# Retention layer: turns, scores, moments and gate products set as steps between the weight units, output units in another order

## The reference, cut to what matters

```python
proj = x @ w_in                            # 1024 -> q 1024, k 1024, v 2048, g 2048
q = rotary(q, pos); k = rotary(k, pos) * dk ** -0.5        # 4 heads of 256
out = decayed_scores(q, k) @ v             # 4 heads of 512, causal, decay by distance
mu, var = mean(out), mean(square(out - mu))                # per token and head
normed = (out - mu) * rsqrt(var + eps) * gn_g
y = silu(g) * normed
return y @ w_out                           # 2048 -> 1024
```

## Times and profile before

| what | value |
|---|---|
| three runs | 2921.59 us median (2919.26 to 2927.62) |
| profiled execution | 2919.76 us, span 2917.9 us |
| PE busy | 2676.1 us, 92% |
| DVE busy | 2125.4 us, 73% |
| ACT busy | 1609.9 us, 55% |
| granted TensorE clock, mean | 0.962 of full speed |
| weights and other data moved | 666 MB, 228 GB/s over the span |

### The profile page before, as it was taken

The page is one execution under the profiler, slowest core; times in us unless marked ns, Lnnn a source line. Parts: engine busy times, 40 slices in busy tenths (PEclk is TensorE's granted clock), DMA queues, the critical chain, the costliest instruction groups (busy, mean ns, idle before and its releaser), DMA issues.

```text
span 2917.9 us, 39530 instructions
## 1 busy us (share of the span) xinstructions
PE 2676.1 (92%) x12842; PEld 2166.2 (74%) x12842; DVE 2125.4 (73%) x2500; ACT 1609.9 (55%) x2092; POOL 19.9 (1%) x37
## 2 busy tenths in 40 slices
PE   3989989988989999998999888699999999999997
PEld 2767768876767787766898667588878877888885
DVE  6766567776656755855545865689989989989998
ACT  2554444445444444433344544477767777777775
POOL 0000000000000000000000000000000000000000
PEclk9999999998999999999999879799999999999999
DMA  6655458755544565644555420599989999999995
GB/s 233 223 155 166 157 180 264 248 188 166 176 146 152 188 194 165 212 130 141 168 180 173 147 80 30 201 333 344 355 300 363 332 351 331 352 342 334 364 358 206
DMA packets 357967, 666.04 MB, mean 228 GB/s; under 512 B 23008, under 2 KB 57312, under 8 KB 357200
## 3 DMA queue, kind: packets, MB, share of 16 engines
q1 hardware_dynamic: 354080, 648.51, 66.2%
q0 software_dynamic: 3760, 15.91, 1.7%
HBM read 663.29 MB, written 1.05 MB: 228 GB/s over the span
## 4 chain that ended last, share of the span: by engine, by line
PE 80%; DVE 8%; ACT 5%; issue 3%; DVEq 2%; DMA 1%; ACTq 0%; SPq 0%
PE ps L451 44%; PE ps L457 22%; DVE wlo L1884 2%; PE ps L471 2%; PE ps L562 2%; ACT whi L1320 1%; PE ps L476 1%; DVE mod_sum L1908 1%; PE ps L1223 1%; PE ps L661 1%; DMA raw<-in_w_ada 1%; DMA ada_raw<-in_w_ada 1%; PE ps L773 1%; DVEq L1907 0%; PE ps L631 0%
## 5 line engine op out<-in xcount | busy, mean ns | idle before, releaser
L1884 DVE TENSOR_TENSOR wlo<-raw,whi 128x1024 fp32r<-128x1024 f32 x709 | 863.5, 1224 | 469.7 <-ACT whi L1320 459.6
L1320 ACT ACTIVATE whi<-raw 128x1024 fp32r<-128x1024 f32 x709 | 746.8, 1059 | 737.8 <-PE ps L457 630.7
L451 PE MATMUL ps<-whi,xh 128*128 128x512 f32 (+3 forms) x1248 | 457.8, 377 | 12.8 <-issue 9.0
L451 PE MATMUL ps<-whi,xl 128*128 128x512 f32 (+3 forms) x1248 | 445.3, 367 | 0.0
L451 PE MATMUL ps<-whi,gathered_hi 128*128 128x512 f32 x896 | 361.8, 404 | 3.4 <-DVE att L2158 2.6
L451 PE MATMUL ps<-whi,gathered_lo 128*128 128x512 f32 x896 | 355.1, 396 | 0.0
L457 PE MATMUL ps<-wlo,xh 128*128 128x512 f32 (+3 forms) x1248 | 294.6, 363 | 0.0
L457 PE MATMUL ps<-wlo,gathered_hi 128*128 128x512 f32 x896 | 283.4, 397 | 5.4 <-DVE wlo L1884 5.4
L451 PEld LDWEIGHTS ps<-whi,xh 128*128 128x128 f32 x1248 | 241.3, 193 | 56.0 <-issue 14.4
L451 PEld LDWEIGHTS ps<-whi,xl 128*128 128x128 f32 x1248 | 241.5, 193 | 37.3 <-issue 1.9
L457 PEld LDWEIGHTS ps<-wlo,xh 128*128 128x128 f32 x1248 | 217.0, 192 | 38.5
(11 more groups left out here) (390 smaller groups left out, 3577.4 us busy)
## 6 DMA issues: line engine op xcount, KB each, us to landing
raw<-in_moe_w_in SPq DMA_DIRECT2D x227, 512.0 KB, 5.5
spare<-in_moe_w_in SPq DMA_DIRECT2D x165, 512.0 KB, 5.7
mod_b<-in_moe_w_out SPq DMA_DIRECT2D x165, 512.0 KB, 5.4
raw<-in_w_ff SPq DMA_DIRECT2D x128, 512.0 KB, 4.6
raw<-in_w_in SPq DMA_DIRECT2D x96, 512.0 KB, 4.0
work<-in_moe_w_in SPq DMA_DIRECT2D x56, 512.0 KB, 5.6
work<-in_moe_w_out SPq DMA_DIRECT2D x56, 512.0 KB, 5.3
raw<-in_w_ada SPq DMA_DIRECT2D x48, 512.0 KB, 4.8
```

Source lines behind the costliest of these rows:

```text
L451: e.matmul(ps[0:lhs[2], banks[t], at:at + width], part[:, k0 + j, t * P:t * P + lhs[2]], whi[:, slot, w], start=first and j == 0 and part ...
L1320: e.activation(whi[:, slot, :], src, ACT.Copy).then_inc(split_hi, 1)
L1884: e.tensor_tensor(wlo[:, slot, :], src, whi[:, slot, :].bitcast(F32), ALU.subtract).then_inc(split_lo, 1)
```

## The change

Nothing of the arithmetic is changed. The instructions of stages 2 and 4 get numbers of weight units behind which they run. With `values` the first v unit, `gated` the first gate unit, `projected` the first output unit:

```diff
+                values = c.n.get("unit", 0) + 16
+                gated, projected = values + 16, values + 32
 PE:
+                at(values + 1, source)
+                at(values + 9, source)
+                for i in range(4):
+                    at(values + 1 + i, wide_turn(0, 2 * i))
+                    at(values + 9 + i, wide_turn(D, 2 * i))
+                at(values + 14, scores)
+                at(gated + 13, source, out_turn(0))
+                at(gated + 14, out_turn(4))
+                at(projected + 4, source, out_turn(8))
+                at(projected + 8, source, out_turn(12))
 ACT:
+                for i in range(4):
+                    at(values + 2 + i, wide_copy(qT, 2 * i))
+                    at(values + 10 + i, wide_copy(kT, 2 * i))
+                at(gated + 8, lambda e: root(e, 8))
+                at(gated + 14, turned(0))
+                at(gated + 15, turned(4))
+                at(projected + 5, turned(0))
+                at(projected + 9, turned(4))
 DVE (the copies and the four turned as in ACT):
+                at(values + 15, decayed)
+                at(gated + 9, inverse)
+                at(gated + 10, gate(0))
+                at(gated + 11, gate(1))
+                at(gated + 14, turned(0), gate(2))
+                at(projected + 1, gate(3))
```

What else changes on PE: `clear` ahead of the turns, ahead of the scores and behind the products with v is gone, and so is ACT's `vec` there. The products with v wait for the chunk before the last only, and for the last one ahead of head 3:

```diff
-                clear(e)
-                chunks_read(e)
...
                 source(e)
+                e.wait_ge(evac_act, c.at("chunk", 1))
+                e.wait_ge(evac_dve, c.at("chunk", 1))
                 for h in range(RET_H):
...
+                    if h == RET_H - 1:
+                        chunks_read(e)
                     job(e, tile0)
                     job(e, tile1)
-                clear(e)
                 for _ in range(4):
                     chunk(e, X, NT, D)
```

The output units come column half 1 first, so that the first unit writes banks 4 and 5, and only the second one waits for ACT's reading of the last gate chunk (banks 2 and 3). SP loads in the same order:

```diff
+RET_OUT = [(kg, n) for kg in range(6) for n in (1, 0)]
...
+                turned(e)
+                for i, (kg, n) in enumerate(RET_OUT):
+                    if i == 1:
+                        chunks_read(e)
+                    if i == 8:
+                        turned(e)
+                    unit(e, Y, NT, kg % 4 * UROWS, (2 + 2 * n, 3 + 2 * n), UCOLS, kg == 0, False)
+                turned(e)
```

More of the change, by code:

```diff
@@ L1039, in retention, with at, wide_turn, fill @@
                 X, Y = (xh, xl, P), (yh, yl, P)
+                values = c.n.get("unit", 0) + 16
+                gated, projected = values + 16, values + 32
+                def at(i, *pieces):
+                    c.weave.setdefault(i, []).extend(pieces)
+                def wide_turn(base, b):
+                    def fill(e, bank):
+                        for j in range(2):
+                            for t in range(NT):
+                                tr = e.transpose(ps[:, bank, (j * NT + t) * P:(j * NT + t + 1) * P],
+                                                 proj[:, t, base + (b + j) * P:base + (b + j + 1) * P], ident)
+                        return tr
+                    return lambda e: side_job(e, fill)
+                def scores(e):
+                    clear(e)
+                    for h in range(RET_H):
+                        for b in range(2):
+                            e.matmul(ps[:, 4 + h // 2, (h % 2) * S:(h % 2 + 1) * S], kT[:, 2 * h + b, 0:P],
+                                     qT[:, 2 * h + b, :], start=b == 0, stop=b == 1)
+                    for h in range(RET_H):
+                        for b in range(2):
+                            mm = e.matmul(ps[:, 7, h * P:(h + 1) * P], kT[:, 2 * h + b, P:S],
+                                          qT[:, 2 * h + b, P:S], start=b == 0, stop=b == 1)
+                    mm.then_inc(score_ready, 1)
+                    c.add("job_d")
+                def out_turn(first):
+                    return lambda e: side_turn(e, lambda t, b: ret_O[:, t, (first + b) * P:(first + b + 1) * P], 4)
+                at(values + 1, source)
[8 more added lines that the diff above has]
+                at(projected + 8, source, out_turn(12))
                 first_chunk(e, lambda t, b: x[:, t, b * P:(b + 1) * P], X)
@@ L1682, in retention, with at, wide_copy, turned @@
             def retention(e):
+                values = c.n.get("unit", 0) + 16
+                gated, projected = values + 16, values + 32
+                def at(i, *pieces):
+                    c.weave.setdefault(i, []).extend(pieces)
+                def wide_copy(dst, b):
+                    return lambda e: jobs(e, [plain(dst[:, b:b + 2, :], lambda bank: ps[:, bank, :].rearrange("p (h s) -> p h s", h=2))])
+                def turned(first):
+                    return lambda e: turn(e, yh[:, first:first + 4, :], 4)
+                for i in range(4):
[6 more added lines that the diff above has]
+                at(projected + 9, turned(4))
                 for side in range(4):
@@ L1696, in retention @@
                     chunk(e, D, read)
[L1697 to L1701, removed]
+                pass_units(e, len(RET_OUT))
                 layer_norm_roots(e, 4)
@@ L2538, in view, with at, wide_copy, turned @@
+                gated, projected = values + 16, values + 32
+                def at(i, *pieces):
+                    c.weave.setdefault(i, []).extend(pieces)
                 def view(t, h):
                     return ret_O[:, t, h * 512:(h + 1) * 512]
+                def wide_copy(dst, b):
+                    return lambda e: jobs(e, [plain(dst[:, b:b + 2, :], lambda bank: ps[:, bank, :].rearrange("p (h s) -> p h s", h=2))])
+                def turned(first):
+                    return lambda e: turn(e, yh[:, first:first + 4, :], yl[:, first:first + 4, :], 4)
@@ L2564, in retention, with inverse @@
[L2564 to L2567, removed]
+                        if i == NT * RET_H - 1:
+                            e.tensor_scalar(st[:, 0:8], st[:, 64:80].rearrange("p (i k) -> p i k", k=2)[:, :, 1], LN_EPS, None, ALU.add)
+                            to_act(e)
+                    return piece
+                def inverse(e):
+                    from_act(e)
+                    e.reciprocal(st[:, 16:24], st[:, 8:16])
+                    e.drain()
@@ new lines, in gate, with piece @@
+                def gate(h):
+                    def piece(e):
+                        chunks_read_by_act(e)
+                        for t in range(NT):
+                            i = h * NT + t
+                            e.scalar_tensor_tensor(view(t, h), view(t, h), st[:, 16 + i:17 + i], ret_V[:, t, h * 512:(h + 1) * 512],
+                                                   ALU.mult, ALU.mult)
+                        if h:
+                            to_pe(e)
+                    return piece
@@ new lines, in retention @@
+                at(projected + 9, turned(4))
+                for side in range(2):
+                    chunk(e, D, copy(proj[:, 1, side * 512:side * 512 + 512]), () if side else (turn_second,))
+                for side in range(2):
+                    chunk(e, D, copy(proj[:, 1, D + side * 512:D + side * 512 + 512]),
+                          [rope_head(0, side, h) for h in range(RET_H)])
+                to_pe(e)
+                for side in range(4):
+                    chunk(e, D, copy(ret_V[:, 1, side * 512:side * 512 + 512]),
+                          [rope_head(D, side, h) for h in range(RET_H)] if side < 2 else ())
+                    if side == 1:
+                        to_pe(e)
@@ L2568, in retention @@
+                jobs(e, [plain(ret_O[:, t, h * 512:(h + 1) * 512], lambda bank: ps[:, bank, :])
+                         for h in range(RET_H) for t in range(NT)])
+                act_copied(e)
+                chunk(e, D, None, [moments(t, h) for h in range(2) for t in range(NT)])
+                chunk(e, D, None, [moments(t, h) for h in range(2, 4) for t in range(NT)])
+                for _ in range(2):
+                    chunk(e, D, None)
+                pass_units(e, len(RET_OUT))
                 e.drain().then_inc(extra_used, 1)
```

45 lines of the change are left out of this document (11 added, 34 removed).

## The result

| | median | runs |
|---|---|---|
| before | 2921.28 us | 4, 2919.26 to 2927.62 |
| changed | 2898.08 us | 4, 2897.06 to 2900.32 |

The medians are 23.2 us apart; the ratio of the two is 0.9917, with a 95% interval of 0.9903 to 0.9931, which is 20 to 28 us. The forecast was 20.3 us less, a median of 2901.3 us, in a range of 2893 to 2911. Timed again beside 15 runs of the kernel before, the changed one stood at 2902.73 against 2922.67, 19.9 us less, ratio 0.9929 (0.9911 to 0.9948). (A sixth execution there took 3763.90 us at a granted clock of 0.66, and is left out.) So the total alone fixes the gain no better than to some microseconds; the layer's own length in the profiles does.

What follows compares the result with a forecast made beforehand. PE sets the pace, standing without weight work for 45.3 us in the retention layer. Savings of 5.4 + 14.9 = 20.3 us give 2899.5 us profiled, 2901.3 us for the median, range 2893 to 2911.

Steps and rivals of the forecast that it cites:

- three places where no weight unit ran on PE: Retention layer: q/k turns to products with v 25.9 us, before the first output unit 14.7, mid-output 4.7; together 45.3.
- rival 1: V stretch: DVE takes PE's place, 3.9 us of gain lost, 2.6 more with table loads; about 2907 us, chance 10%.
- rival 3: More than counted: turns at PE's pace 0.7 less, 0.4 wait gone, clock dip up to 6.8; 2894 us, chance 6%.
- v part: Turns of q and k, scores, decays and products with v: 25.9 us becomes 20.5, saving 5.4 us.
- gate and output part: Root, gate products and output turns: 19.4 us becomes 4.5, saving 14.9 us, the clock's 1.7 included.
- the turn's price: Transposes placed between weight units on PE: 1.02 us for eight, read from a row of the first block.
- the place ahead of the output: Before the first output unit: PE waits 0.4 us for the last turns' subtractions; bounds nothing to 2.8 us.
- Scores and decays: Behind v unit 14: scores stay 5.4 us; decay products, 1.9 us on DVE, hide beside v unit 15's 2.79.
- rival 4: Short waits lower PE's clock, each later unit 1.7 us more; slower than before, up to 2939 us, chance 2%.
- C: Place ahead of the ninth output unit, 1369.78 to 1374.46, where PE multiplies no weights: 4.7 us.
- 2 (given back later): Late weight loads or clock dips in the layer norm and later stages lose the saving: 2908 us, chance 8%.
- 5: A piece waits for one behind it in another queue, so engines still run in series: 2920 us, chance 4%.

## Why the prediction was right

**The sum.** It named three places where no weight unit ran on PE, and what of each would stay. The medians, 2898.08 and 2902.73, stand on either side of the forecast of 2901.3; that they stand so near is partly luck, since totals of one kernel scatter by ten. The lengths are the test. Three of its sums are loose by less than 2 us, without effect on the forecast: the 45.3 us "in which PE multiplies no weights" hold the 1.7 by which an output unit was slow, rival 1 adds up to 2907.8 and not 2907, rival 3 to 2893.4 and not 2894. By place:

| | forecast | measured | by what |
|---|---|---|---|
| v part | 5.4 | 6.2 | v parts 73.3 and 67.1 |
| gate and output part | 14.9 | 15.2 | 59.4 + 46.7 against 47.2 + 43.7 |
| layer | 20.3 | 21.4 | |

**The term that was mis-sized is the turn's price.** "1.02 us for eight transposes" was in truth 0.44 x 2 = 0.88. The timeline of the v part of the changed kernel:

```profile
1221.04 0.60 PE L1052 MATMUL ps<-const,proj 128*128 128x128 f32 x4
...
1221.40 0.48 PE L452 MATMUL ps<-whi,xh 128*128 128x512 f32 x1
...
1224.28 0.60 PE L1052 MATMUL ps<-const,proj 128*128 128x128 f32 x4
...
1224.63 0.47 PE L452 MATMUL ps<-whi,xh 128*128 128x512 f32 x1
```

Unit starts are 3.23 apart, 0.44 more than a unit. The stretch that I had read in the first block had a wait in it, as the row ahead of its second turn shows in the kernel before:

```profile
822.33 1.09 PE L457 MATMUL ps<-wlo,xh 128*128 128x512 f32 x4
823.37 1.07 PE L607 MATMUL ps<-const,proj 128*128 128x128 f32 x8
```

PE was free at 822.33 + 0.93 = 823.26 and turned at 823.37, 0.1 of the 0.14 too much. Sixteen groups of four at 0.07 less are 1.1 us. The forecast was short by 1.1 in all, but two smaller misses stand in that: the scores took 0.2 less than forecast, and the place ahead of the output 0.3 more, as the first output unit stood 0.55 behind the last gate unit and took 0.1 longer than others, against a forecast wait of 0.4. The run with one transpose of four shows that the price is the transposes' own.

**Scores and decays.** In the changed kernel:

```profile
1260.90 3.62 PE L1062 MATMUL ps<-qT,kT 128*128 128x256 f32 x16
...
1264.35 1.95 PE L1066 MATMUL ps<-qT,kT 128*128 128x128 f32 x16
1266.06 0.47 PE L452 MATMUL ps<-whi,xh 128*128 128x512 f32 x1
1266.34 1.22 DVE L2574 SCALAR_TENSOR_TENSOR att<-ps,mod_a 128x1024 f32<-128x1024 f32 x1 [2.86 <-PE ps L1066]
...
1267.48 0.68 DVE L2575 SCALAR_TENSOR_TENSOR att<-ps,mod_a 128x512 f32<-128x512 f32 x1
...
1268.93 1.02 PE L1092 MATMUL ps<-att 128*128 128x512 f32 x2
```

The scores take 1266.06 - 1260.90 = 5.2 us (forecast 5.4); both products with the decays are done by 1268.16, 0.8 us before PE asks, and PE goes on without a wait, as the forecast had it. The 0.2 here and eight groups at 0.07 are the 0.8 us of the v part.

**The waits.** "`source` should be there 0.5 us early":

```profile
1243.98 0.69 DVE L2551 COPY att<-ps 128x512 f32<-128x512 f32 x1
...
1245.17 0.60 PE L1052 MATMUL ps<-const,proj 128*128 128x128 f32 x4
```

DVE ends at 1244.67, PE turns at 1245.17. The run with the k turns one unit (2.8) earlier waited 2.3 and 2.1, so the room is 0.5 to 0.7 and no more. "PE waits 8.0 - 7.6 = 0.4 us" ahead of the output is the one row of 0.4 above.

**What was wrong is the argument against rival 4.** The forecast said that waits up to 2.0 leave the clock alone and that it fell only at the wait of 6.0. Inside the layer that holds for both profiles of the kernel before. Outside it, the same trace already says otherwise. Behind the layer, at the layer norm:

```profile
1399.99 0.36 PE L471 MATMUL ps<-whi,xh 128*128 128x256 f32 x1 [1.99 <-DVE xl L1967]
```

```profile
1400.00:1410.00 10.00, 7.94 (x52) 7.73 (x53) 8.64 (x12) 2.24 (x4) 1.10 (x2) 0.83 0.49 158
```

A wait of 1.99 us, and the clock is at the lower level for 3.4 us from 1400.54. In the experiments it also fell behind the waits of 3.2, 2.3 and 2.1, behind the one of 2.0 with the turns in series in one profile of two, and behind the two waits at C in the one profile with the gate products in series but in neither of the kernel before. It did no harm, as the changed kernel has a single wait of 0.4 in the layer and the clock stayed up in both its profiles. The forecast came out right because it had the waits right, not because short waits are harmless: as the k turns one unit earlier show, with `source` late by 2.3 there the clock's 1.7 would have come on top. In the Trainium skill (TensorE: Matmul & The Clock Gate, A second HAM failure mode: psum-queue depth-cycling) short idles between groups of matmuls made one kernel's clock go back and forth. These traces agree for waits of about 2 us, which the forecast had not granted; each such fall cost 1.7 us under load and did not last.

**Rivals.** 1 (DVE takes PE's place) was 0.5 us away and did not come; of ACT's two further table loads PE's waits show nothing. 2 (given back later): behind the layer the changed kernel took 0.9 more in the first pair of profiles and 2.8 more in the second, within what that part scatters by. That nothing at all is given back there is not shown. 3 (more than counted) came true in its first term, the turns at PE's own pace. 5 is excluded by the stretches. The change does each thing it says. The new place of the moments was not tried by itself; PE has no wait that would show it.

## What to carry to other kernels

Where one engine sets the pace, list the stretches in which it does no streaming work, and price each by what must stay on that engine; what is left goes once steps stand between units that cover their partners' latency. Place a step by the moment when its last operand is done: here 0.5 us of room at the k turns held, and one unit earlier cost 4 us, 1.7 of them clock. To read such a change, measure between fixed instructions inside the profile: here they repeated within 0.2 us, except where one execution had a fall of the clock and the other had none, while the totals scatter by ten. Before a rule on the clock is used against a rival, look for its exceptions in the whole trace, not only in the stages that change.

## What the runs showed of the hardware

The clock's fall is not a function of the wait alone. A PE wait of 2.0 us in one program was followed by 3.4 us at the lower clock in one execution and by none in the next; waits of 2.3 and 2.1 by 3.4 us each; one of 3.2 with one of 1.5 behind it by 6.8 us; one of 6.0 or 6.1 by 13.7 us in all three profiles that had it. Each 3.4 us under load cost 1.7 us. So a wait of 2 us on PE has cost up to 3.7 us.

Waits that no experiment touches stand in all thirteen profiles, and can be counted. A wait of 2.15 to 2.17 us in the first block, between 374 and 379 us and again between 933 and 939, was followed by a fall in 19 of 26 cases. The wait of 1.95 to 2.00 in the layer norm behind the layer was followed by one within 2 us of its end in 10 of 13. One of 1.57 to 1.58, at about 1155 us, was followed by none in 13.

A transpose of 128x128 between two streams of 512-column matmuls costs 0.11 us of PE, with no sum for the switch: a step of one transpose cost 0.11, one of four 0.44, one of eight 0.87.
